# Two stick-breaking heads per step, hgrn stages regrouped and the weave's turns redistributed, in a two-block transformer kernel on one core

## The reference, cut to what matters

```python
z = einsum(q, k) * scale
log_rest = where(mask, log_sigmoid(-z), 0.0)
between = (reverse cumulative sum of log_rest over the keys, shifted by one)
a = where(mask, exp(log_sigmoid(z) + between), 0.0)
o = einsum(a, v)
```

## Time and profile before

| | us |
|---|---|
| median of 3 runs (lowest, highest) | 1131.92 (1131.5, 1131.95) |
| the profiled execution's own time | 1132.12 |
| its span, first to last instruction | 1130.3 |
| PE busy | 1079.4 (96% of the span) |
| DVE busy, ACT busy | 591.5 (52%), 460.3 (41%) |
| mean granted TensorE clock | 0.99 of full |

### The profile page before, as it was taken

One profiled execution on the slowest core, in us unless ns is written; L12 is line 12 of the kernel. 1 busy time (PEld: TensorE's weight loads), 2 busy tenths in 40 slices (PEclk: granted clock), 3 DMA queues, 4 the chain that ended last, 5 costly groups with the idle time before them and its releaser, 6 DMA issues.

```text
span 1130.3 us, 14044 instructions
## 1 busy us (share of the span) xinstructions
PE 1079.4 (96%) x5524; PEld 861.7 (76%) x5524; DVE 591.5 (52%) x1132; ACT 460.3 (41%) x836; POOL 39.9 (4%) x49
## 2 busy tenths in 40 slices
PE   4999999999999999999999999999999989999894
PEld 4887788888878888888888888997776656666583
DVE  4246644334365666533666635528576743666744
ACT  4334432232254444411444424534346346556622
POOL 0000000000011000000000001100000001000004
PEclk9999999999999999999999999999999899999997
DMA  6311122322332723431223233431120124211011
GB/s 238 107 62 56 58 75 93 112 94 93 116 110 90 288 94 95 147 113 38 93 94 108 81 101 121 167 118 57 57 66 19 38 66 165 96 38 38 19 38 75
DMA packets 28625, 105.51 MB, mean 93 GB/s; under 512 B 3226, under 2 KB 3386, under 8 KB 27920
## 3 DMA queue, kind: packets, MB, share of 16 engines
q1 hardware_dynamic: 24576, 85.15, 23.0%
q0 software_dynamic: 3696, 18.42, 4.7%
q10 hardware_dynamic: 288, 1.05, 0.2%
HBM read 99.86 MB, written 7.36 MB: 95 GB/s over the span
## 4 chain that ended last, share of the span: by engine, by line
PE 82%; issue 7%; DVE 5%; ACT 4%; DMA 2%; POOL 0%; POOLq 0%; ACTq 0%; DVEq 0%; SPq 0%
PE ps L666 24%; PE ps L668 23%; PE ps L667 23%; PE ps L1019 1%; PE ps L1036 1%; PE ps L1053 1%; PE ps L782 1%; ACT whi L1086 1%; ACT A L1355 1%; PE ps L756 1%; PE ps L683 1%; DVE wlo L1434 1%; PE ps L767 1%; DMA GR<-brow 1%; PE ps L916 1%
## 5 line engine op out<-in xcount | busy, mean ns | idle before, releaser
L666 PE MATMUL ps<-XH,whi 128*128 128x512 f32 (+1 forms) x880 | 342.1, 389 | 4.4 <-ACT whi L1086 3.2
L668 PE MATMUL ps<-XH,wlo 128*128 128x512 f32 (+1 forms) x880 | 331.5, 377 | 0.0
L667 PE MATMUL ps<-XL,whi 128*128 128x512 f32 (+1 forms) x880 | 330.9, 376 | 0.0
L1434 DVE TENSOR_TENSOR wlo<-raw,whi 128x1024 fp32r<-128x1024 f32 (+2 forms) x159 | 190.7, 1205 | 225.7 <-ACT whi L1086 225.2
L1086 ACT CAST whi<-raw 128x1024 fp32r<-128x1024 f32 (+2 forms) x159 | 162.6, 1027 | 95.1 <-PE ps L668 68.8
L666 PEld LDWEIGHTS ps<-XH,whi 128*128 128x128 f32 x880 | 167.3, 190 | 42.2 <-issue 8.0
L668 PEld LDWEIGHTS ps<-XH,wlo 128*128 128x128 f32 x880 | 167.1, 190 | 30.4
L667 PEld LDWEIGHTS ps<-XL,whi 128*128 128x128 f32 x880 | 167.5, 190 | 27.1 <-issue 0.2
L666 PE MATMUL ps<-whi,GH 128*128 128x512 f32 x176 | 68.8, 391 | 0.0
L668 PE MATMUL ps<-whi,GL 128*128 128x512 f32 x176 | 68.5, 389 | 0.0
L667 PE MATMUL ps<-wlo,GH 128*128 128x512 f32 x176 | 68.5, 389 | 0.0
(11 more groups left out here) (250 smaller groups left out, 1354.2 us busy)
## 6 DMA issues: line engine op xcount, KB each, us to landing
raw<-wp SPq DMA_DIRECT2D x151, 512.0 KB, 3.4
vec_dram<-row_dram POOLq DMA_DIRECT2D x1, 3072.0 KB, 13.4
x_dram<-H POOLq DMA_DIRECT2D x1, 2048.0 KB, 8.0
A<-w1c POOLq DMA_DIRECT2D x2, 1024.0 KB, 6.5
A<-x_dram POOLq DMA_DIRECT2D x1, 2048.0 KB, 12.8
y<-A SPq DMA_DIRECT2D x8, 256.0 KB, 2.0
raw<-wp SPq DMA_DIRECT2D x4, 402.0 KB, 3.6
A<-vec_dram POOLq DMA_DIRECT2D x1, 1536.0 KB, 9.4
```

Source lines behind the costliest of these rows:

```text
L666: self.e.matmul(o, ah, bh, start=start, stop=False)
L667: self.e.matmul(o, ah, bl, start=False, stop=False)
L668: return self.e.matmul(o, al, bh, start=False, stop=stop)
L1434: self.e.tensor_tensor(wlo[BUF[i]][:, 0:w], raw[i % NR][:, 0:w], whi[BUF[i]][:, 0:w].bitcast(F), ALU.subtract).then_inc(sems["lo"], 1)
```

## The change

Stick-breaking goes by pairs p = 0, 1 (heads 2p and 2p+1, index j = 0, 1) and no longer by single heads. Head j keeps bank 5 or 7. s_first issues both heads' products one behind the other (they take rows 0 to 63 and 64 to 127), then ACT makes Abs, Abs, Exp, Exp, Ln, Ln; s_pv issues the eight matmuls by turns j = 0, 1 into the two halves of the output partitions of bank 5, and one copy of 128 partitions replaces two of 64. `SPb` gets a second row, and the scratch `AA` of both heads, which now also holds what `EE` held, lies in freed places of `HG` and others; so ACT's s_first waits for pair 0 of hgrn. s_first and s_second of a block stand two turns apart, and the next s_first one turn behind s_second. The first s_first of the second pair waits for the first pair's copy out of bank 5 (semaphore s_o).

hgrn's second half of the preparation (prep1, mult0) moves ahead of the first `h_off`, which gets a turn of its own behind diag. The compression gets two empty turns after `c_blk` and one before `c_end`. The rates become 57/52, 28/26 and 16/17. `nsa_begin` also waits for `kct` before it loads `Y`.

```diff
@@ -396,9 +396,10 @@
             en.h_q1(p)
             en.h_prep(p, 0)
             yield
-            en.h_off(p, 0)
             en.h_prep(p, 1)
             en.h_mult(p, 0)
+            yield
+            en.h_off(p, 0)
             yield
             en.h_off(p, 1)
             yield
@@ -422,24 +423,28 @@
         for i in range(2):
             en.c_blk(i)
             yield
+            yield
+            yield
             for l in range(4):
                 en.c_mm(i, l)
                 yield
+        yield
         en.c_end()
         yield
 
     def stick():
-        for h in range(4):
-            for n in range(5):
-                if n < 4:
-                    en.s_first(h, n)
-                if n > 0:
-                    en.s_second(h, n - 1)
+        for p in range(2):
+            for n in range(4):
+                en.s_first(p, n)
                 yield
-            en.s_pv(h)
+                yield
+                en.s_second(p, n)
+                yield
             yield
-
-    weave(projections(), (hgrn(), 4, 45 / 54), (stick(), 33, 24 / 26), (compress(), 42, 11 / 16))
+            en.s_pv(p)
+            yield
+
+    weave(projections(), (hgrn(), 4, 57 / 52), (stick(), 33, 28 / 26), (compress(), 42, 16 / 17))
...
-        SPb = region(0, 1, 1280)
-        AA = region(1280, 1, 1280)
+        SPb = region(0, 2, 1280)
...
-        EE = [Hf[:, 3712:4096], region(2560, S)]
...
+        AA = [[region(G0 + at, S - 128 * kb) for kb, at in enumerate((0, 512, 896, 1152))],
+              [region(2560, S), Hf[:, 3712:4096], region(G0 + 1280, 256), sm2[:, 72:200]]]
...
+            def s_first(self, p, n):
+                kb = 3 - n
                 cs = slice(kb * 128, S)
+                for j in range(2):
+                    r = slice(64 * j, 64 * j + 64)
+                    self.wait_ge("sq2", p + 1)
+                    self.wait_ge("sk2", p + 1)
+                    self.wait_ge("avv", 4)
+                    if n == 0 and j == 0:
+                        self.wait_ge("s_o", p)
+                    else:
+                        self.wait_ge("s_e", 2 * max(4 * p + n - 1, 0) + (j + 1 if p or n else 0))
+                    self.e.matmul(ps[STICK[j]][:, cs], SK[r, p, kb * 128:kb * 128 + 128], SQ[r, p, cs],
+                                  start=True, stop=False, skip_group_check=True).then_inc(sems["z1"], 1)
...
+            def s_pv(self, p):
+                self.wait_ge("s_f", 8 * p + 8)
                 for kb in range(4):
+                    for j in range(2):
+                        at = 256 + (2 * p + j) * 64
+                        f = self.e.matmul(ps[STICK[0]][64 * j:64 * j + 64, kb * 128:S], AV[:, kb, at:at + 64],
+                                          AA[j][kb], start=(kb == 0), stop=(kb == 3), skip_group_check=True)
                 f.then_inc(sems["s_av"], 1)
...
+            def s_first(self, p, n):
+                kb, at = 3 - n, 4 * p + n
+                cs = slice(kb * 128, S)
                 self.wait_ge("qz", 1)
                 self.wait_ge("mc", N_MC)
+                self.wait_ge("h_m", 21)
+                self.wait_ge("h_dg", 2)
+                self.wait_ge("s_av", p)
+                for j in range(2):
+                    self.wait_ge("z1", 2 * at + j + 1)
+                    self.e.activation(AA[j][kb], ps[STICK[j]][:, cs], ACT.Abs).then_inc(sems["s_l"], 1)
+                for j in range(2):
+                    self.wait_ge("s_l", 6 * at + 1 + j)
+                    self.e.activation(AA[j][kb], AA[j][kb], ACT.Exp, scale=-1.0).then_inc(sems["s_l"], 1)
+                for j in range(2):
+                    self.wait_ge("s_l", 6 * at + 3 + j)
+                    self.e.activation(AA[j][kb], AA[j][kb], ACT.Ln, bias=1.0).then_inc(sems["s_l"], 1)
...
+            def s_pv(self, p):
+                self.wait_ge("s_av", p + 1)
+                self.e.copy(OTS[:, 3 + p, :], ps[STICK[0]][:, :]).then_inc(sems["s_o"], 1)
...
             def nsa_begin(self):
-                self.wait_ge("s_o", 4)
+                self.wait_ge("s_o", 2)
                 self.wait_ge("s_r", 8)
...
                 self.wait_ge("h_pr", 21)
+                self.wait_ge("kct", 2)
```

More of the change, by code:

```diff
@@ L1386, in s_second @@
-            def s_second(self, h, n):
-                kb, at = 3 - n, 4 * h + n
-                self.wait_ge("z2", at + 1)
-                self.wait_ge("s_av", h)
-                self.e.activation(cols(AA, 0, kb, kb * 128), ps[STICK[(5 * h + n) % 2]][:, kb * 128:S],
-                                  ACT.Exp).then_inc(sems["s_e"], 1)
-            def s_pv(self, h):
-                r = slice(64 * (h % 2), 64 * (h % 2) + 64)
-                self.wait_ge("s_av", h + 1)
-                self.e.copy(OTS[r, 3 + h // 2, :], ps[STICK[h % 2]][r, :]).then_inc(sems["s_o"], 1)
+                self.wait_ge("h_m", 21)
@@ L1398, in mix_tile, with s_second @@
+            def s_second(self, p, n):
+                kb, at = 3 - n, 4 * p + n
+                for j in range(2):
+                    self.wait_ge("z2", 2 * at + j + 1)
+                    self.e.activation(AA[j][kb], ps[STICK[j]][:, kb * 128:S], ACT.Exp).then_inc(sems["s_e"], 1)
+            def s_pv(self, p):
+                self.wait_ge("s_av", p + 1)
+                self.e.copy(OTS[:, 3 + p, :], ps[STICK[0]][:, :]).then_inc(sems["s_o"], 1)
             def mix_tile(self, n):
@@ L1812, in s_second @@
-            def s_second(self, h, n):
-                kb, at = 3 - n, 4 * h + n
-                if n in (1, 2):
-                    tail = cols(SPb, 0, kb, kb * 128 + 128)
-                    self.wait_ge("z2", at + 1)
-                    self.wait_ge("s_r", 2 * h + n - 1)
-                    self.e.tensor_tensor(tail, tail, cols(SPb, 0, kb + 1, kb * 128 + 128), ALU.add
-                                         ).then_inc(sems["s_r"], 1)
-                diag = AA[:, 0, OFF[kb]:OFF[kb] + 128]
-                self.wait_ge("s_e", at + 1)
-                self.e.tensor_tensor(diag, diag, STR, ALU.mult).then_inc(sems["s_f"], 1)
+                for j in range(2):
+                    self.wait_ge("s_l", 6 * at + 5 + j)
+                    self.wait_ge("z2", 8 * p)
+                    self.e.scalar_tensor_tensor(cols(SPb, j, kb, kb * 128), ps[STICK[j]][:, cs], 0.0, AA[j][kb],
+                                                ALU.max, ALU.add).then_inc(sems["s_d"], 1)
@@ new lines, in s_first, with s_second @@
+                for j in range(2):
+                    diag = SPb[:, j, OFF[kb]:OFF[kb] + 128]
+                    self.wait_ge("s_d", 4 * at + 1 + j)
+                    self.e.tensor_tensor(diag, diag, STR, ALU.mult).then_inc(sems["s_d"], 1)
+            def s_second(self, p, n):
+                kb, at = 3 - n, 4 * p + n
+                if n in (1, 2):
+                    for j in range(2):
+                        tail = cols(SPb, j, kb, kb * 128 + 128)
+                        self.wait_ge("z2", 2 * at + j + 1)
+                        self.wait_ge("s_r", 4 * p + 2 * (n - 2) + j + 1 if n > 1 else 0)
+                        self.e.tensor_tensor(tail, tail, cols(SPb, j, kb + 1, kb * 128 + 128), ALU.add
+                                             ).then_inc(sems["s_r"], 1)
+                for j in range(2):
+                    diag = AA[j][kb][:, 0:128]
+                    self.wait_ge("s_e", 2 * at + j + 1)
+                    self.e.tensor_tensor(diag, diag, STR, ALU.mult).then_inc(sems["s_f"], 1)
```

69 lines of the change are left out of this document (16 added, 53 removed).

## The result

| | us |
|---|---|
| changed kernel, median of 5 runs (lowest, highest) | 1136.34 (1135.23, 1138.18) |
| kernel before, median of 5 runs beside them | 1131.76 (1131.5, 1131.95) |
| ratio, 95% interval | 1.0043 (1.0029 to 1.0058) |
| profiled execution of the changed kernel: own time, span | 1137.48, 1135.6 |

A forecast was written before the change was run, and what follows sets the result against it. PE, busy 96% of the span, was taken as the bound. Work -9.9, old waits -13.3, old half clock -5.2, new waits +28.15, new half clock +4.8 gave +4.55, so 1136.5 us; range 1126.5 to 1144, forecast's own 1133 to 1141.

The forecast's parts named there:

- new waits: PE waits added across hgrn's three pairs, the stick and the exit: 5.4 + 5.6 + 8.9 + 7.6 + 0.65 = 28.15 us.
- new half clock: PE at 1.2 GHz behind three new waits of 2.5 us or longer: 4.8 us, bounds 0 and 14 us.
- First h_off 1.2, 1.35 and 1.4 us: PE waits at off0 of hgrn pairs 0, 1 and 2, with one quarter between diag and off0.
- Second h_off 0.6 and 0.95 us: PE waits at off1 of hgrn pairs 1 and 2 for copies queued behind other ACT work.
- Doubled step 24, 2.9 us: hgrn pair 1, L3 and L4 in one step: PE waits 2.9 us for wlo and a DVE round.
- pv2, 4.05 us: hgrn step 41: last pick queued behind s_first (0,2), 6.85 us against PE's 2.8 us; longest wait, 4.05 us.
- s_second (0,3), 2.2 us: Stick: PE waits 2.2 us for six 512-column ACT passes, two sums and a mask, against two quarters.
- The compression costs nothing: Compression's additions no longer cost PE anything, as three turns lie between them and its first product.
- DVE stays a level ahead: Rival: DVE and ACT overlap better, three long waits lose 4.7 us; -4.9 us, 1127 us; chance 0.24.
- Much slower: Rival: four waits each followed by 3.5 us lost at 1.2 GHz, little hidden; 1144 us; chance 0.11.
- My waits, but full clock: Rival: predicted waits with full clock throughout; -0.25 us, 1131.7 us; chance 0.20.
- Pairs don't run side by side: Rival: each product waits for its own semaphore, so the 9.9 us are not saved; 1146 us; chance 0.04.

The follow-up runs named there:

- regroup_only: Kernel before with the stick pairs and hgrn regrouped as in the change, at rate 48/54, compression's turns old: 1120.03 us, ratio 0.9893.
- swap_early: Changed kernel with POOL's two small SRX transfers issued ahead of the 1 MB W1 load: 1129.95 us, ratio 0.9992.
- fillers: Changed kernel with idle products on PE, read by no one, ahead of seven waits: 1128.38 us, ratio 0.9976.
- pairs_alone: Changed kernel with hgrn's and the compression's turns and rates put back (45/54, 11/16), stick still by pairs: 1121.29 us, ratio 0.9914.
- compress_only: pairs_alone with only the compression's empty turns and rate of 16/17 from the change: 1121.66 us, ratio 0.9908.
- rate_only: pairs_alone with hgrn's rate at 53/52 in place of 45/54: 1135.44 us, ratio 1.0047.
- regroup_swap: regroup_only with POOL's small SRX transfers issued ahead of the 1 MB W1 load: 1114.61 us, ratio 0.9856.
- turns_alone: Kernel before, single heads, with only hgrn's and the compression's new turns and rates and the kct wait: 1135.88 us, ratio 1.0038.

## Why the prediction was right, and where it was not

1136.5 us was predicted and 1136.34 measured, slower and inside the forecast's own 1133 to 1141. The sum stands on five terms. Two of them, PE's work and the old half clock, both end as PE's busy time and are measured as one; here they are as the weaves of the profiled executions have them:

| term | predicted | measured |
|---|---|---|
| PE work of the pairs, and old half clock | -9.9 - 5.2 = -15.1 | -17.2 (busy 178.3 to 161.1, regroup_only at full clock) |
| old waits go | -13.3 | -11.7 (all of PE's idle time) |
| new waits | +28.15 | +22.9 (the same) |
| new half clock | +4.8 | +11.2 (busy 172.3 against 161.1) |
| sum | +4.55 | +5.2; the medians differ by 4.6 |

**Errors cancel.** The new waits came out 5.3 us smaller than predicted, the old ones 1.6 us smaller, and the busy time that goes 2.1 us larger; the new half clock came out 6.4 us larger, more than twice its term. The side was right, and for the most part the kinds of wait were the ones named; that the number is right to 0.2 us is luck. By its terms it is good to about 6 us.

The smaller errors have sources that the trace shows. The "about 2 us of waits under 0.35 us" ahead of the change are not there: 11.3 us are listed and PE stands for 11.7 in all. The -5.3 us for s_first were a lower bound by columns; measured are 12.66 - 6.89 = 5.8 us, as a head's small products take longer than their share of columns. s_pv gave 6.1 us with the half clock at it, about 4.8 us without, against 4.6. And product 5 of pair 2, by the prediction's own numbers, is 7.1 - 3.7 - 1.05 = 2.35 us and not 2.5.

**A reading error stands in the record.** The table of the new order of stages, printed ahead of the prediction, puts prep1 and mult0 into the turn of diag. The diff has a `yield` ahead of them: they have a turn of their own, hgrn has 45 turns and not 42, and every hgrn stage from pair 0's prep1 on stands one to three steps later than in the table. The true order of pair 2 is diag 33, prep1 and mult0 34, both halves of h_off in 35, levels 36 to 42, last pick 43, value product 44. The stick and the compression stand as printed. Nearly all hgrn places in the prediction are off by this, and it goes with most of the misses by name:

- *First h_off 1.2, 1.35 and 1.4 us*: none. With the extra turn two quarters lie between diag and h_off, and DVE is done in time. This is the largest term that was not there, 3.95 us.
- *Second h_off 0.6 and 0.95 us ("this is what moving prep1 ahead of off0 costs")*: 2.23 and 4.17 us. The mechanism was named and the size was off by four: the prediction counted ACT's own work ahead of the copies, but not that one exponential in it waits in turn for DVE behind `wlo`. In pair 2 both halves stand in one step, which the false table hid.
- *Doubled step 24, 2.9 us*: 2.02 us at that step; in truth it holds levels 1 and 2. Right in kind and place, but it is the one wait of over 2 us with full clock behind it, where 0.5 was foretold.
- *pv2, 4.05 us, "does not depend on what came before it"*: the chain (s_first of two heads, six ACT passes, `wlo`, picks) is right step by step and cost 3.60 us, but it fell upon product 5, as the stage that stands behind it in the true order. pv2 waited 2.73 us, behind the next s_first.
- *s_second (0,3), 2.2 us*: none. In the true order it stands in step 44 right behind pv2, whose 2.73 us are a wait for the same burst. One burst was charged twice.
- *First product of stick pair 1, 0.65 us*: 0.69. *Exit, 0.65 us*: 0.47.
- *The compression costs nothing*: 3.29 us. The step counted turns between the additions and the product and not what the additions wait for: a transfer that POOL's own queue holds behind a 1 MB load. swap_early shows what it is worth here, 6.4 us with its share of the clock.

**Clock.** This is the term that failed in size. Predicted were 7.8 us at most behind three waits, less 3 us hidden: 4.8. There were five waits of 2.2 us and more with half clock behind each, four windows at 0.86, 28 us at half; at full effect that is 14 us. PE's busy time shows 11.2 us of it, and the kernel fillers got 8.0 back by the medians.

**The rivals.** "DVE stays a level ahead" would need waits plus half clock under 28.4 us: they were 22.9 + 11.2 = 34.1. "Much slower" had the clock better than the forecast, four waits with the longer stretch of half clock behind each, 13 us with little of it hidden; its 1144 us did not come because the waits were 5.3 us smaller than both took them. "My waits, but full clock" (1131.7 us) is nearly the kernel fillers, which ran at 1128.38; that case was real, though not this kernel's. "Pairs don't run side by side" is refuted by 1.06 us a pair and by pairs_alone.

**What the prediction did not see** is that the loss is in one number. It went by stages and so had all three edits of the turns as one; pairs_alone, regroup_only, compress_only and rate_only give -10.1 us for the pairs, -1.3 for the grouping, +0.4 for the compression's turns and +14.2 for the rate. The pairs make ACT and DVE work come in bursts, six passes at a time, and that costs little as long as few stages of the lane that PE needs each step are queued behind the bursts: in pairs_alone PE stands only 1.8 us longer than before.

The three parts of the turns add up to 13.3 us, against 15.0 for all together; the 1.7 us between are within the intervals. What stays open: what the rate does by packing hgrn's levels and what by their place beside the stick, which no run here parts, and why the clock falls behind one wait and not behind another of the same length.

## What to carry to other kernels

When several lanes share in-order queues, batching one lane's work shortens PE's part and lengthens the block of work that every other lane on ACT and DVE must stand behind; keep the lanes that PE needs each step away from it (here by 45/54 in place of 53/52, worth 14 us) before counting the gain. Write down the order of stages by running through the yields of the new code, one by one, for one overlooked yield moved most of hgrn's waits to another instruction than predicted. Check each term of such a sum by itself, the waits against all of PE's idle time and the clock against its busy time: here errors of 2 to 6 us hid in a sum that came out right. For each wait look one step further back than the engine that is named: at what the last thing in that queue was itself waiting for (an exponential behind DVE, a small transfer behind a large one).

## What the runs showed of the hardware that was not expected

- **More work on PE made the kernel faster.** Idle products in seven waits took 8.0 us off (1136.34 to 1128.38 us), the granted clock of the weave's windows going from four at 0.86 to 1.00 throughout. The idle products themselves kept PE busy for 16.8 us.
- **The length of one wait does not decide the clock.** A wait of 2.23 us was followed by 0.50 in the changed kernel and by 1.00 in regroup_swap; one of 2.02 us by 0.50 in turns_alone and by 1.00 in the changed kernel (each in the 4 us window behind it). What else decides was not tried.
- **One program doesn't always get the same clock.** The kernel before ran from 1128.31 us (mean granted clock 0.991) to 1133.47 us (0.986) in 18 runs beside the first experiments, though its first five lay within 0.45 us; regroup_only ran twice at 1118.0 us (0.993) and twice at 1122 us (0.986). Few runs close together don't show how far a kernel spreads.
- **Two fp32 products of 64 rows, or into 64 output partitions each, take one's time**: 1.06 us against 1.05 for 512 columns, and 2.37 us against 2.3 for 1280 columns.
